# Loading the two sliding-window caches from ScalarE's DMA queue instead of GpSimd's, in a decoder-step kernel

## The reference, cut to what matters

```python
def swa_sample(q, k, v, buf_k, buf_v, sink):
    kk = jnp.concatenate([buf_k, k], axis=1)
    vv = jnp.concatenate([buf_v, v], axis=1)
    ...
    scores = jnp.einsum('bqkgd,bskd->bkgqs', qg, kk).astype(jnp.float32) * (Dh ** -0.5)
    ...
    o = jnp.einsum('bkgqs,bskd->bqkgd', p.astype(vv.dtype), vv).reshape(B, T, H * Dh)
    return o, kk[:, -WINDOW:], vv[:, -WINDOW:]
```

## Time and profile before

| | |
|---|---|
| median of 3 runs | 1082.15 us |
| the profiled execution: its time | 1081.09 us |
| its span | 1079.2 us |
| PE busy | 971.2 us (90%) |
| DVE, ACT, POOL busy | 525.7, 352.5, 253.3 us |
| mean granted TensorE clock | 0.941 |
| DMA | 203.73 MB, mean 189 GB/s |

### The profile page before, as it was taken

One profiled execution on the slowest core, in us unless ns is written; L12 is line 12 of the kernel. 1 busy time (PEld: TensorE's weight loads), 2 busy tenths in 40 slices (PEclk: granted clock), 3 DMA queues, 4 the chain that ended last, 5 costly groups with the idle time before them and its releaser, 6 DMA issues.

```text
span 1079.2 us, 17824 instructions
## 1 busy us (share of the span) xinstructions
PE 971.2 (90%) x6998; PEld 600.4 (56%) x6998; DVE 525.7 (49%) x1069; ACT 352.5 (33%) x879; POOL 253.3 (23%) x281
## 2 busy tenths in 40 slices
PE   7979999998999998999999298999899877999994
PEld 6866788887445756633333156657558563333331
DVE  0346630467657668143332555684188583243227
ACT  2325531121001623233342243554215332333323
POOL 2220710051500001535311115500000015451121
PEclk9999999999989997999999599899999976999997
DMA  9422361072207235989998503441236155999976
GB/s 325 107 91 57 85 189 63 17 196 79 68 0 187 93 155 200 386 332 408 403 415 307 187 1 87 91 149 40 66 131 274 39 190 203 347 399 411 417 198 157
DMA packets 81467, 203.73 MB, mean 189 GB/s; under 512 B 22666, under 2 KB 47922, under 8 KB 72288
## 3 DMA queue, kind: packets, MB, share of 16 engines
q1 hardware_dynamic: 60832, 151.31, 38.6%
q0 software_dynamic: 19952, 49.05, 14.7%
q10 hardware_dynamic: 592, 2.13, 0.5%
HBM read 184.46 MB, written 25.92 MB: 195 GB/s over the span
## 4 chain that ended last, share of the span: by engine, by line
PE 76%; DVE 11%; DMA 5%; ACT 4%; issue 3%; POOL 1%; SPq 0%; POOLq 0%; DVEq 0%; ACTq 0%
PE PS L1600 15%; PE PS L1408 11%; PE PS L1046 9%; PE PS L1147 6%; PE PS L1615 6%; PE PS L1431 3%; PE PS L1111 3%; ACT arena L1973 2%; DMA x<-y_tok 2%; PE PS L1034 2%; PE PS L1069 2%; PE PS L1817 2%; PE PS L1742 2%; PE PS L1589 2%; PE PS L1827 2%
## 5 line engine op out<-in xcount | busy, mean ns | idle before, releaser
L1973 ACT ACTIVATE arena<-PS 32x520 f32<-32x520 f32 (+9 forms) x150 | 73.7, 504 | 186.7 <-PE PS L1046 42.1
L1600 PE MATMUL PS<-ring,arena 128*32 128x512 f32 x648 | 116.9, 592 | 1.4 <-DVE arena L3020 1.4
L1600 PE MATMUL PS<-arena 128*32 128x512 f32 x648 | 111.2, 603 | 2.9 <-issue 1.8
L1046 PE MATMUL PS<-xT,ring 128*128 128x260 f32 x416 | 93.6, 385 | 3.7 <-DVE arena L2452 2.3
L3036 DVE COPY arena<-PS 128x256 f32<-128x256 f32 x24 | 10.2, 425 | 169.9 <-PE PS L1608 169.9
L1046 PEld LDWEIGHTS PS<-xT,ring 128*128 128x128 f32 x416 | 78.3, 190 | 18.4 <-DVE arena L2452 4.3
L810 POOL TENSOR_TENSOR rstd<-rstd,small 128x1 f32<-128x1 f32 (+1 forms) x25 | 16.3, 651 | 272.2 <-DVE rstd L2740 244.2
L2250 ACT ACTIVATE arena<-PS,lnc 128x128 f32<-128x128 f32 x192 | 69.5, 471 | 23.0 <-PE PS L1589 22.9
L1615 PE MATMUL PS<-ring,arena 128*32 128x512 f32 x432 | 69.0, 595 | 1.2 <-DVE arena L3036 1.2
L1147 PE MATMUL PS<-ring,xT 128*128 128x256 f32 (+2 forms) x336 | 66.8, 361 | 0.0
L1034 PE MATMUL PS<-ident,x 128*128 128x128 f32 (+1 forms) x240 | 38.5, 312 | 28.9 <-DVE x L2816 20.9
(11 more groups left out here) (431 smaller groups left out, 1862.5 us busy)
## 6 DMA issues: line engine op xcount, KB each, us to landing
arena<-in_moe_w_in_dram SPq DMA_DIRECT2D x27, 1024.0 KB
ring<-in_moe_w_in_dram SPq DMA_DIRECT2D x27, 1024.0 KB, 9.8
ring<-in_moe_w_out_dram SPq DMA_DIRECT2D x18, 1024.0 KB, 16.9
ring<-in_w_in_even_dram SPq DMA_DIRECT2D x11, 1024.0 KB, 9.0
xT<-in_moe_w_in_dram SPq DMA_DIRECT2D x10, 1024.0 KB
arena<-in_moe_w_out_dram SPq DMA_DIRECT2D x8, 1024.0 KB
xT<-in_moe_w_out_dram SPq DMA_DIRECT2D x6, 1024.0 KB
y_tok<-in_c_zeros_dram POOLq DMA_DIRECT2D x8, 512.0 KB, 10.7
```

What stands on the lines that cost most here:

```text
L1046: mm = pe.matmul(o[out_rows, 512 * h:512 * h + HALF], lhs(k), rhs(k)[:, HALF * h:HALF * h + HALF], start=(k == 0), stop=(k == nk - 1))
L1600: mm = pe.matmul(o[group(q), 0:512], xT_[:, k, group(q)], w(q, k), start=(k == 0), stop=(k == KD - 1), **quarter(q))
L1973: return act.activation(dst, src, ACT.Copy)
```

## The change

The loop that loads the two caches leaves POOL's stream. ACT issues the same two transfers: the keys' right behind `swap(0)`, the values' right behind `swap(1)`. The semaphore, its count and all waits on it stay.

```diff
--- before.py
+++ after.py
@@ -913,8 +913,6 @@
             load(qdec[:, :, :], io["c_qdec"], "const_in")
             load(rope_t[:, :, :], io["c_rope"], "const_in")
 
-            for dst, name in ((Kw, "cache_swa_k"), (Vw, "cache_swa_v")):
-                load(dst[0:127, :, :], io[name][0, :, 1:128].rearrange("b s h d -> s b (h d)"), "cache_in")
             load(gng[:, 0, :], io["ret_gn_g"][0].partition_broadcast(P), "gn_in")
             load(gng[:, 1, :], io["ret_gn_b"][0].partition_broadcast(P), "gn_in")
             for c, name in enumerate(("ln_g", "ln_b")):
@@ -2032,6 +2030,9 @@
 
             for i in range(5):
                 swap(i)
+                if i in (0, 1):
+                    dst, name = ((Kw, "cache_swa_k"), (Vw, "cache_swa_v"))[i]
+                    act.dma_start(dst[0:127, :, :], io[name][0, :, 1:128].rearrange("b s h d -> s b (h d)")).then_inc(s["cache_in"], 16)
             act.wait_ge(s["rope_done"], 5)
             for kv in range(2):
                 ins = copy(kaD[64 - 64 * kv:128 - 64 * kv, kv, :], kaD[64 * kv:64 * kv + 64, kv, :])
```

## The result

| | before | after |
|---|---|---|
| median | 1082.22 us (4 runs beside the change) | 1099.71 us (4 runs, 1098.83 to 1101.60) |
| ratio, 95% interval | | 1.0163 [1.0144, 1.0182] |
| span of the profiled execution | 1079.2 us | 1096.9 us |
| mean granted TensorE clock | 0.941 | 0.934 |

The kernel became slower by 17.5 us (1099.71 - 1082.22). The direction was the forecast one; the predicted 1121 us was 21 us too high.

The account below looks back on a forecast made before the run. PE was taken to bound the kernel, with a stop at 74.5 caused by POOL's issue. ACT's holds (+45) less the stop (-6), clock 0, gave +39 us on 1081.1: 1120, 1121 us for the median; range 1073 to 1142.

Parts of the forecast that it names:

- What bounds the kernel: PE carries 76% of the chain; its stop from 74.5 to 81.6 comes from POOL's values' issue holding DVE's negation.
- the gain: Around PE's stop at 74.5: -6.05 us for DVE's hold, -1.5 for the half clock after it, together -7.6.
- "not held" rival: At ACT's two issues: the queue takes a whole transfer as one order, only the gain remains, 1074.5 us; chance 0.27.
- First by the keys' issue, then by the values': Behind swap(0) and swap(1): both issues hold ACT, 65 us together, moving PE's qr 0 from 58.84 to 103.8.
- likeliest case: ACT held twice, by both cache issues: 65 us of hold, 1121 us, own range 1100 to 1144; chance 0.55.
- held-once rival: At ACT: keys' issue returns at once, values' waits until the keys are handed over; 1084 us (1075 to 1095); chance 0.13.
- theory B: From the experiments, not the prediction: ACT's queue has room for a fixed number of runs, some 1130, whatever the orders.
- 824 runs: 27 + 4 us: At ACT's values' issue, if held once: 1016 - 192 runs must go, so the hold ends at about 55.
- the pieces that come later are in the 33 ns already: On the caches' DMA engine: 33 ns a run already includes later pieces, since they passed under POOL's transfers too.
- They cost nothing earlier as well: POOL's loads behind the caches, some 85 us earlier: may hold DVE 0 to 1.5 us in all, taken as 0.
- The clock: At PE after ACT's hold: having stood some 40 us, PE gets the half clock anyway, so 0 in the sum.
- The cover: During ACT's hold: PE runs through qa 3 and ka, stops shortly for va, stands before kaTok; later stretches swallow nothing.

Follow-up runs that it names:

- put-back: Keys' cache on ACT and values' on POOL, with POOL's values' issue put behind DVE's first negation; 1080.94 us, ratio 1.0013 to the kernel before.
- the cures: The six versions without the long hold on ACT and without the old stop of PE; 1074.2 to 1077.6 us.
- e_values_late: The changed kernel with the values' issue moved from behind swap(1) to behind ACT's copy of qr 0; 1074.47 us, ratio 0.9921.
- e_values_late_again: The changed kernel with the values' issue behind ACT's copy of qr 0, timed again in more rounds; 1076.37 us, ratio 0.9939.
- e_values_only: The changed kernel with the keys' cache back on POOL; ACT issues only the values', behind swap(1); 1075.91 us, ratio 0.9953.
- e_two_parts_apart: The changed kernel with each cache on ACT as 112 and 15 partitions, the values' pair behind swap(2); 1076.27 us, ratio 0.9940.
- e_keys_in_three: The changed kernel with the keys' cache in three ACT transfers (43, 43, 41 rows), the values' in one, later; 1088.92 us, ratio 1.0082.
- e_pool_112_15: The kernel before, both caches still on POOL, each as transfers of 112 and 15 partitions; 1077.56 us, ratio 0.9974.
- e_keys_only: The changed kernel with the values' cache back on POOL; ACT issues only the keys', behind swap(0); 1074.22 us, ratio 0.9952.

## Why the prediction was right or wrong

**What bounds the kernel, and the gain: right.** The stop at 74.5 had its cause in POOL's issue; the put-back shows it. Its price was read as -6.05, and PE got -5.87; the half clock after it as -1.5, measured -1.40. Together I took -7.6; by PE's timeline from `qr` 0 to the first use of the caches the cures gain 106.22 - 99.69 = 6.53 us (before 165.06 - 58.84; e_values_late 158.84 - 59.15). The step missed is the next wait: 0.74 us given back at L2453 of the kernel after, where PE waits for the rotation. The runs gain less still, 5.1 us in e_values_late_again (1081.45 - 1076.37). A part of that is a half clock that comes in some executions: it costs 1.69 us at 90 in e_values_only and in e_two_parts_apart, and as much in the first projections of e_values_late_again, which took 36.99 us there and 35.30 in the kernel before. The rest is not traced. The "not held" rival, 1074.5 or a ratio of 0.993, lies at the edge of what the cures reach, 1074.2 to 1077.6, mostly at 0.994 to 0.995.

**"First by the keys' issue, then by the values'": the step that failed.** The likeliest case had both issues hold ACT, 65 us in all. The keys' returned in 0.54 us. The mistake was to read the 4.11 and 2.92 us of SP as a queue with room for three pieces, 192 runs an engine. The held-once rival named the other reading, each issue waits for the order before it, and was set aside because "I find no row that needs that"; it got a chance of 0.13. The orders of 344 runs show that reading right: 108 runs outstanding at each return, 114 in the kernel after, and no more than one order waiting. Rows 8 alone could not have told the two apart, since both pieces are of one size; the chances ought to have been nearer to each other.

The objection to that reading, "then the queue would take only two pieces", fails as well, and SP's queue in the kernel before shows it. Its DMA section, from 0 to 10.66 (piece 2's issue returns), to 13.62 (piece 3's) and to 28 (all five pieces have gone):

```profile
q1 hardware_dynamic: 1032, 2.50, 67.1%
...
q1 hardware_dynamic: 2053, 3.53, 76.3%
...
q1 hardware_dynamic: 5932, 7.44, 81.6%
```

A piece is 1024 runs and 16 semaphore writes, 1040 packets. So 5932 - 3 x 1040 = 2812 packets stood before piece 2, and 1780 of them were left when its issue returned: 111 for each of sixteen engines. Before piece 3 they were 3852 - 2053 = 1799, or 112. It is the same number as on ACT's queue, for runs of 1 KB; the third piece on top of it (64 runs) is what the prediction counted as room for three. One room for everything would have to be 111 + 65 = 176 packets an engine here and 1130 runs in the kernel after, so these rows speak against theory B too.

**The held-once rival's own time: too low.** It gave 1084 us, up to 1095, with the hold ending at about 55. It ended at 68.52. Its formula from there was right: 68.63 + 13.0 = 81.6, measured 81.73. What failed is "824 runs: 27 + 4 us". First, 902 runs had to go, not 824, for only 114 were still to go when the issue returned. Second, the run's price: 33 ns came from the landings of before, "the pieces that come later are in the 33 ns already". But in the kernel after, the engine is also asked for POOL's small loads, and from 28 to 36 it moved 45 runs, 178 ns each; before 28, beside the last pieces and POOL's first loads, only 24. From 36 to 68.5 it moved the other 833 or so (902 less the 69 that had gone by 36) at 39 ns, beside pieces; alone, from 70 to 80, 27 ns each (10 us for 370).

**"They cost nothing earlier as well": wrong.** Of POOL's loads that moved forward I costed only what they could do to DVE. On the DMA engine they cost 8.1 us of hold; kept back, `qr` 0 starts 7.4 us earlier (81.73 - 74.31) and the ratio falls from 1.0163 to 1.0119, 4.8 us; the rest is within the scatter named above.

**The clock: half right.** I took 0, since the half clock comes back after a long stop anyway. It did: +2.06 for the new one against -1.40 for the old one. The long stop was read as some 40 us; it was 23.05.

**The cover: right.** PE went on through `qa` 3, `ka` and `va` while ACT was held, and stopped before `kaTok`; the short stop before `va` did not come, for `swap(1)` had run before the hold (with the keys in three orders it came, 9.70 us). Later stretches swallowed nothing (+18.41 at the first use of the caches, +17.7 in the span). POOL's wait for the caches ended at 100.15, long before `kwT`.

Put together with the measured terms, the prediction's own sum is 22.89 - 5.87 + 2.06 - 1.40 + 0.74 = 18.4.

## What to carry to other kernels

Before a transfer is given to an engine's queue, ask what stands before it in that queue and how many runs that puts on the fullest DMA engine: the second issue holds its engine until the first order has been handed over (here, until some 110 of its runs were left), and everything behind it in the instruction stream waits too. Count the partitions: a cache of 127 moved at one engine's pace, parts of 112 and 15 landed in 6.5 to 8.7 us instead of some 40, and that cured the same kernel without a change of queue. And when a slow transfer is moved, look at what it used to hold back, for that now competes with it.

## What the runs showed of the hardware

- The second of two issues on ACT returned with 114, 110, 108, 108 and 115 runs of the order before it still to go, with orders of 1016 and 344 runs, after holds of 40.50, 32.42, 21.60 (with the first issue), 12.76 and 1.72 us. On SP's queue, with orders of 64 runs of 1 KB for each engine, it was 111 and 112 packets an engine. Behind piece 0 and the larger runs of the input (4 KB) it was 85 (409 packets gone by 6.51, when piece 1's issue returned), so the number may depend on the runs. Why it is that number was not tried.
- A DMA issue on POOL of 6.7 us held a negation of 128 x 4 on DVE for 6.22 and 5.89 us, but not rotations of 128 x 520 (0.70 us). With 112 and 15 partitions the issue takes about 0.74 us, and in e_pool_112_15 the negations took 0.17 us. What POOL does in those 6.7 us was not tried.
- Two caches from two queues slow each other, as on one DMA engine, and not evenly. With the keys on ACT's queue and the values on POOL's (e_keys_only), ACT's queue had moved 552 packets by 85, where in the kernel after all 1016 of the keys' had gone by 72 (1034 in all); the values on POOL took 49.6 us to land, against 38.3. From 60 to 70 both queues moved 33 packets, which were 0.14 MB of POOL's and 0.02 MB of ACT's. (From 36 to 50 the counts were 1480 and 174, so it isn't always packet for packet; why is open.) Nothing held ACT, and PE did not wait for the late caches. POOL's and ACT's queue in e_keys_only, from 60 to 70:

```profile
q0 software_dynamic: 33, 0.14, 4.3%
...
q10 hardware_dynamic: 33, 0.02, 0.8%
```
- The half clock after a wait of 1.9 us came in some executions and not in others, and so it did after the wait of about 1 us for piece 0 (in e_values_late_again, 1.00 us, and not in e_keys_in_three, 1.10 us); what decides it is open.
